# The recurrence of an RWKV-7 mixer in one Trainium2 kernel: factor matmuls laid on four quarters of the array, copies of T moved to ScalarE, factor steps two pairs ahead, the two directions interleaved phase by phase

## The reference

```python
def step(state, inp):
    r_t, w_t, k_t, v_t, kk_t, a_t = inp
    sk = jnp.einsum('bhij,bhj->bhi', state, kk_t)
    state = (state * w_t[:, :, None, :]
             - sk[..., :, None] * (kk_t * a_t)[:, :, None, :]
             + v_t[..., :, None] * k_t[:, :, None, :])
    y = jnp.einsum('bhij,bhj->bhi', state, r_t)
    return state, y
...
_, ys = lax.scan(step, s0, xs, reverse=reverse)
...
y = y + wkv7_scan(rh, hs(decay), kd, vh, kk, ah, reverse=(d == 1))
```

## Time and profile before

| | us |
|---|---|
| median of 3 runs (2830.68 to 2834.61) | 2833.74 |
| the profiled execution, its own time | 2847.62 |
| its span, first to last instruction | 2845.8 |
| mean granted TensorE clock, as a share of full | 0.963 |
| busy: TensorE / VectorE / ScalarE / POOL | 2624.5 / 1603.1 / 1137.7 / 917.4 |
| the recurrence, from its first transpose to its last step | 456 |

### The profile page before, as it was taken

One profiled execution on the slowest core, in us unless ns is written; L12 is line 12 of the kernel. 1 busy time (PEld: TensorE's weight loads), 2 busy tenths in 40 slices (PEclk: granted clock), 3 DMA queues, 4 the chain that ended last, 5 costly groups with the idle time before them and its releaser, 6 DMA issues. The chain is left out here.

```text
span 2845.8 us, 54939 instructions
## 1 busy us (share of the span) xinstructions
PE 2624.5 (92%) x23187; PEld 2156.2 (76%) x23187; DVE 1603.1 (56%) x2296; ACT 1137.7 (40%) x1802; POOL 917.4 (32%) x625
## 2 busy tenths in 40 slices
PE   5998999796999998979999999996897999999998
PEld 5776566576889988758888888885776888888887
DVE  7775522467565544666555565445655555556445
ACT  4211332553434332344444443554434444444434
POOL 1302122104112110225777770000412777773000
PEclk9999999898999998989999999998998999999999
DMA  6676433602211221322222227553122322225654
GB/s 232 229 270 214 168 133 155 205 18 80 76 47 48 82 80 32 126 72 76 89 75 81 89 90 276 171 169 109 53 90 73 89 89 74 82 89 216 190 182 144
DMA packets 295927, 346.48 MB, mean 122 GB/s; under 512 B 28383, under 2 KB 224212, under 8 KB 295684
## 3 DMA queue, kind: packets, MB, share of 16 engines
q1 hardware_dynamic: 286044, 336.64, 36.6%
q10 hardware_dynamic: 9640, 6.33, 0.7%
HBM read 271.58 MB, written 71.34 MB: 120 GB/s over the span
## 5 line engine op out<-in xcount | busy, mean ns | idle before, releaser
L2848 POOL TENSOR_TENSOR cg_u_lo<-cg_u_raw,cg_u_hi 128x512 fp32r<-128x512 f32 x210 | 314.9, 1507 | 147.2 <-ACT cg_u_hi L2734 147.2
L131 PE MATMUL cg_ps<-m_hi,cg_u_hi 128*128 128x512 f32 x844 | 331.1, 392 | 25.9 <-DVE cg_u_lo L2923 21.6
L133 PE MATMUL cg_ps<-m_hi,cg_u_lo 128*128 128x512 f32 x844 | 330.3, 391 | 0.0
L132 PE MATMUL cg_ps<-m_lo,cg_u_hi 128*128 128x512 f32 x808 | 315.8, 391 | 0.0
L2734 ACT ACTIVATE cg_u_hi<-cg_u_raw 128x512 fp32r<-128x512 f32 x216 | 132.1, 629 | 380.7 <-PE cg_ps L133 230.0
L131 PEld LDWEIGHTS cg_ps<-m_hi,cg_u_hi 128*128 128x128 f32 x844 | 159.8, 189 | 61.0 <-DVE cg_u_lo L2923 22.4
L131 PE MATMUL cg_ps<-over_y_tx,cg_u_hi 128*128 128x512 f32 x480 | 186.7, 389 | 0.0
L132 PE MATMUL cg_ps<-over_y_tx,cg_u_hi 128*128 128x512 f32 x480 | 186.7, 389 | 0.0
L133 PE MATMUL cg_ps<-over_y_tx,cg_u_lo 128*128 128x512 f32 x480 | 186.7, 389 | 0.0
L133 PEld LDWEIGHTS cg_ps<-m_hi,cg_u_lo 128*128 128x128 f32 x844 | 159.6, 189 | 33.5
L2900 DVE SCALAR_TENSOR_TENSOR cg_z<-cg_ps,top_conv_f,cg_z 128x1023 f32<-128x1023 f32 x88 | 112.9, 1283 | 115.3 <-ACT cg_z L2758 115.3
(11 more groups left out here) (475 smaller groups left out, 6515.2 us busy)
## 6 DMA issues: line engine op xcount, KB each, us to landing
cg_u_raw<-in_ffn_up SPq DMA_DIRECT2D x88, 512.0 KB, 5.1
cg_u_raw<-in_ffn_down SPq DMA_DIRECT2D x64, 512.0 KB, 5.0
qkv_mw<-in_ada_w SPq DMA_DIRECT2D x12, 2048.0 KB
over_f_d_raw<-in_ffn_down SPq DMA_DIRECT2D x48, 512.0 KB, 5.4
scr_act<-cg_z SPq DMA_DIRECT2D x44, 512.0 KB, 2.7
qkv_mw<-in_ada_w SPq DMA_DIRECT2D x8, 1024.0 KB, 11.3
next_w<-in_mix_in SPq DMA_DIRECT2D x16, 512.0 KB, 6.2
za_out<-in_ada_w SPq DMA_DIRECT2D x8, 1024.0 KB
```

The source lines that it names most:

```text
L131: nc.tensor.matmul(out, a_hi, b_hi, start=first, stop=False)
L132: nc.tensor.matmul(out, a_hi, b_lo, start=False, stop=False)
L133: return nc.tensor.matmul(out, a_lo, b_hi, start=False, stop=last)
L2848: G.tensor_tensor(u_lo[:, n % RING], source(g, i), u_hi[:, n % RING].bitcast(F32), ALU.subtract).then_inc(ulo_done, 1)
```

## The change

Every function gets a guard that makes it empty for a pair number outside 0 to 7 (left out below). The two heads of a tile get different homes: `home(c, u)` is `side(c)` for the units of head 0 and `other(c)` for those of head 1. X, values write to `home` from `side` or `other`; T and solve read at `home` and write to `side`; U reads and writes at `home`. PSUM is seen in units of 128 columns: X and T use `wide(g, 0)` (banks 0 and 1), U `wide(g, 1)` (banks 2 and 3), with head 0 in the first bank and head 1 in the second. Loops run over f, then hh, then c. Since U1 of head 1 is now needed at the other half, `lower` computes it once more there and VectorE copies it under a mask; `upper` is left with head 0. The alphas of head 1 lie in the other order, so VectorE makes them in two instructions.

```diff
+        pw = pb[:, :, :].rearrange("p k (f n) -> p (k f) n", n=P)
...
-        def alpha_of(g, m):
-            a = halves(st[m % 2][g][:, :, 0:P])
-            return a[:, :, ::-1, :] if g == 0 else a[:, :, :, ::-1]
+        def alpha_of(g, m, hh):
+            a = halves(st[m % 2][g][head(hh), :, 0:P])
+            a = a if g == 0 else a[:, :, :, ::-1]
+            return a[:, :, ::-1, :] if g == hh else a
+
+        def alpha_slot(c, hh):
+            return slice(((1 - c) ^ hh) * CH, (((1 - c) ^ hh) + 1) * CH)
+
+        def home(c, u):
+            return side(c) if u < KU else other(c)
+
+        def wide(g, r):
+            return pw[:, (2 * g + r) * UN:(2 * g + r + 1) * UN, :]
 
         def rho_of(g, m):
             a = st[m % 2][g][:, :, P:2 * P]
...
-        def narrow(g, k, b):
-            return bank(g, k)[:, 0:UN * HC].rearrange("p (u q b) -> p u q b", u=UN, b=b)
+        def narrow(g, r, b):
+            return wide(g, r)[:, :, 0:HC].rearrange("p u (q b) -> p u q b", b=b)
...
+            def load_lw(g, m):
+                if m < NPAIR:
                     sp.wait_ge(f_alpha[g], m)
+                    load(lw[g], lw_d[g][:, :, tokens_of(g, m)], rates_loaded[g])
+                    sp.wait_ge(f_nb[g], m)
+                    load(kk[g], kk_d[:, :, tokens_of(g, m)], f_loaded[g])
+
+            def load_aa(g, m):
+                if m < NPAIR:
                     sp.wait_ge(f_nbeta[g], m)
-                    sp.wait_ge(f_kd[g], m)
...
+            for m in range(-1, NPAIR):
+                if 0 <= m < NPAIR - 1:
+                    for g in range(2):
+                        if m:
+                            sp.wait_ge(rg_c[g], 2 * m)
+                        load_values(g, m + 1)
+                load_lw(0, m + 2)
+                load_aa(1, m + 2)
+                load_rx(1, m + 2)
+                load_lw(1, m + 2)
+                load_kx(1, m + 2)
+                load_aa(0, m + 2)
+                load_rx(0, m + 2)
+                load_kx(0, m + 2)
             for g in range(2):
                 for done in (f_alpha, f_nbeta, f_kappa, f_rho, f_ends):
                     sp.wait_ge(done[g], NPAIR)
...
                 for f in range(KU):
                     for c in range(2):
                         for hh in range(2):
                             nbeta = t[head(hh), f, 2 * P + CH + c * CH:2 * P + CH + (c + 1) * CH]
-                            ins = mm(bank(g, hh)[side(c), f * CH:(f + 1) * CH], t[head(hh), f, (1 - c) * CH:(2 - c) * CH], nbeta,
+                            ins = mm(bank(g, hh)[side(c), f * CH:(f + 1) * CH], t[head(hh), f, alpha_slot(c, hh)], nbeta,
                                      start=True, stop=True)
+                for f in range(KU):
+                    for c in range(2):
+                        nbeta = t[head(1), f, 2 * P + CH + c * CH:2 * P + CH + (c + 1) * CH]
+                        ins = mm(bank(g, 1)[other(c), (KU + f) * CH:(KU + f + 1) * CH], nbeta, t[head(1), f, alpha_slot(c, 1)],
+                                 start=True, stop=True)
                 ins.then_inc(l_done[g], 1)
 
...
                 pe.wait_ge(tok_c[g], 5 * m + 5)
-                for u in range(UN):
-                    hh, f = divmod(u, KU)
-                    for c in range(2):
-                        ins = mm(bank(g, 2)[side(c), u * CH:(u + 1) * CH], xn[g][other(c), hh, 2 * f + c, 0:CH], wv[g][other(c), c, u, :],
-                                 start=True, stop=True)
+                for f in range(KU):
+                    for hh in range(2):
+                        u = hh * KU + f
+                        for c in range(2):
+                            ins = mm(bank(g, 2 + hh)[home(c, u), f * CH:(f + 1) * CH], xn[g][other(c), hh, 2 * f + c, 0:CH],
+                                     wv[g][other(c), c, u, :], start=True, stop=True)
                 ins.then_inc(mv_done[g], 1)
 
...
-                for u in range(UN):
-                    hh, f = divmod(u, KU)
-                    for c in range(2):
-                        out = bank(g, 3)[side(c), u * HC:(u + 1) * HC].rearrange("p (q b) -> p q b", b=b)
-                        ins = mm(out, xn[g][side(c), hh, 2 * f + c, 0:CH], cols1(src[side(c), u, :], b, 0), start=True, stop=True)
+                for f in range(KU):
+                    for hh in range(2):
+                        u = hh * KU + f
+                        for c in range(2):
+                            out = wide(g, 0)[home(c, u), u, 0:HC].rearrange("p (q b) -> p q b", b=b)
+                            ins = mm(out, xn[g][side(c), hh, 2 * f + c, 0:CH], cols1(src[side(c), u, :], b, 0), start=True, stop=True)
                 ins.then_inc(x_done[g], 1)
 
-            def level_tu(g, m, i):
...
+                for f in range(KU):
+                    for hh in range(2):
+                        u = hh * KU + f
                         for c in range(2):
                             if i == 0:
-                                out, x = bank(g, 0)[side(c), u * CH:(u + 1) * CH], XL[i][g][side(c), u, :]
+                                out, x = wide(g, 0)[side(c), u, 0:CH], XL[i][g][home(c, u), u, :]
                             else:
-                                out = bank(g, 0)[side(c), u * HC:(u + 1) * HC].rearrange("p (q b) -> p q b", b=b)
-                                x = cols1(XL[i][g][side(c), u, :], b, 0)
-                            ins = mm(out, old[side(c), u, :], x, start=True, stop=True)
-                    ins.then_inc(t_done[g], 1)
+                                out = wide(g, 0)[side(c), u, 0:HC].rearrange("p (q b) -> p q b", b=b)
+                                x = cols1(XL[i][g][home(c, u), u, :], b, 0)
+                            ins = mm(out, old[home(c, u), u, :], x, start=True, stop=True)
...
+                            out, y = wide(g, 1)[home(c, u), u, 0:CH], old[home(c, u), u, :]
                         else:
-                            out = bank(g, 1)[side(c), u * HC:(u + 1) * HC].rearrange("p (q b) -> p q b", b=b)
-                            y = cols1(old[side(c), u, :], b, 1)
-                        ins = mm(out, XL[i][g][side(c), u, :], y, start=True, stop=True)
+                            out = wide(g, 1)[home(c, u), u, 0:HC].rearrange("p (q b) -> p q b", b=b)
+                            y = cols1(old[home(c, u), u, :], b, 1)
+                        ins = mm(out, XL[i][g][home(c, u), u, :], y, start=True, stop=True)
                 ins.then_inc(u_done[g], 1)
 
...
-                for u in range(UN):
-                    hh, f = divmod(u, KU)
-                    for c in range(2):
-                        ins = mm(bank(g, 2 + hh)[side(c), f * P:(f + 1) * P], U[g][side(c), u, :], rz[g][side(c), u, :],
-                                 start=True, stop=True)
+                for f in range(KU):
+                    for hh in range(2):
+                        u = hh * KU + f
+                        for c in range(2):
+                            ins = mm(bank(g, 2 + hh)[side(c), f * P:(f + 1) * P], U[g][home(c, u), u, :], rz[g][home(c, u), u, :],
+                                     start=True, stop=True)
                 ins.then_inc(z_done[g], 1)
 
...
```

T and U become phases of their own, `step` is cut in `step_open` (what doesn't depend on the state) and `step_close`, `turn` and `scores` in two parts each; `level_t` of VectorE is dropped and ScalarE has it. TensorE's order:

```diff
-            for m in range(NPAIR):
-                for phase in (turn, scores, lower, values):
-                    for g in range(2):
-                        phase(g, m)
-                for i in range(NL):
-                    for g in range(2):
-                        level_x(g, m, i)
-                    for g in range(2):
-                        level_tu(g, m, i)
-                for phase in (solve, carry):
-                    for g in range(2):
-                        phase(g, m)
-                for c in range(2):
-                    for g in range(2):
-                        step(g, m, c)
+            for m in range(NPAIR + 1):
+                turn(0, m, 0)
+                turn(1, m, 0)
+                turn(0, m, 1)
+                step_close(1, m - 1, 1)
+                scores(0, m, 0)
+                scores(0, m, 1)
+                turn(1, m, 1)
+                scores(1, m, 0)
+                lower(0, m)
+                scores(1, m, 1)
+                values(0, m)
+                level_x(0, m, 0)
+                lower(1, m)
+                level_t(0, m, 0)
+                level_u(0, m, 0)
+                level_x(0, m, 1)
+                values(1, m)
+                level_x(1, m, 0)
+                level_t(0, m, 1)
+                level_u(0, m, 1)
+                level_t(1, m, 0)
+                level_u(1, m, 0)
+                level_x(1, m, 1)
+                level_x(0, m, 2)
+                level_t(1, m, 1)
+                level_t(0, m, 2)
+                level_u(1, m, 1)
+                level_x(1, m, 2)
+                level_u(0, m, 2)
+                level_t(1, m, 2)
+                level_x(0, m, 3)
+                level_u(1, m, 2)
+                level_t(0, m, 3)
+                level_x(1, m, 3)
```

(115 more changed lines are left out.)

317 lines of the change are left out of this document (202 added, 115 removed).

## The result

The changed kernel takes 2870.2 us (median of 4 runs, 2863.0 to 2879.7), the kernel before, run beside it, 2834.2; the ratio is 1.012 [1.010, 1.015]. The forecast was 2753.

A forecast was written before the change was run, and what follows sets the result against it. TensorE's issue was taken as the bound: 22 us later start, 1.5 cold start, 1.1 last close and eight pairs of 43.9 make 375.8 for 456.0, 80 less; with the median's offset 2753, range 2725 to 2795.

The forecast's parts named there:

- PE's rate: TensorE issue: each quarter takes an instruction each 55 to 60 ns; four quarters give 14 ns where two give 29.
- term of -10.0 us a pair: PE issue per pair: values 0.9, X 4.7, T 3.8, solve 1.5 less, `lower` 0.9 more.
- the prediction's pair: One pair of the recurrence: best 54.4 less 10.0, less 1.5, plus 1.0 is 43.9 us, bounds 41 and 48.
- three signs of being wrong: X or T groups staying at 1.03 us, a pair over 48 us, or a start costing under 10 us.
- The floor as a rival: Issue floor between 14 and 29 ns in the four-quarter phases: 4.8 us a pair, 38 in all, 2791; chance 0.04.
- rule of the Trainium skill: TensorE start-to-start never below about 25 ns; values, X and T stay 11 ns above `lower`'s rate, result 2809.
- rule on weight loads: Loads overlap only when row group differs; T and solve keep their rate: 42 us, 2795; chance 0.06.
- Clock: Mean pair's excess over the best, 2.6 us, goes without the hole ahead of T; otherwise up to 2 us a pair.
- Idle time and the order: Waits in a pair: other direction's phases cover copies, so idle falls from 3.5 to 2.0 us, 1.5 less.
- Latency as a rival: PE waits at ScalarE's or VectorE's copies, half a us at ten level phases: +5 a pair, 2793; chance 0.14.
- Factor steps and T copies: ScalarE 25.6, VectorE about 29 us a pair, free beside PE; lost cover costs 0.5 us on each engine.
- The start: Iteration -1 precedes pair 0's first copies: first masked scores at 692, start 22 us later, bounds 14 and 28.

The follow-up runs named there:

- e1: TensorE streams alone, two or four quarters, 32 to 128 columns; with 64 columns on four, 128 loads each 3.45 us, 27 ns a load.
- e9: TensorE streams alone on four quarters, with no-operations or 24 transfers of 512 KB beside; 128 loads each 6.2 us beside transfers, 3.45 without.
- e6_places4: e5_places with the factors on four quarters and the added instructions of `lower`; 2842.4 us, 1.001 of the kernel before.
- e5_places: Changed kernel with factors on two quarters, alphas in old order, factor steps one pair ahead at earlier, reordered places; 2824.5 us, 0.995 of the kernel before.
- e4_quarters: Kernel before with the factors on four quarters and what `lower` needs; order, T copies and factor steps as before; 2846.4 us, 1.003.
- e8_t_act: Kernel before with the T copies moved from VectorE to ScalarE, nothing else; 2838.2 us, 1.001.
- e10_t_dve: e5_places with the T copies back on VectorE, nothing else; 2857.5 us, 1.007 of the kernel before.
- e2_two: Changed kernel with factors back on two quarters, without the added `lower` work; order, T copies, two pairs' notice stay; 2844.9 us, 1.002 of the kernel before.
- e7_order: e2_two with the alphas of the second head in their old order; 2847.1 us, 1.004 of the kernel before.

## Why the prediction was wrong

**PE's rate.** This is the step that failed: "So a quarter takes an instruction each 55 to 60 ns ... and the number of quarters in use sets the rate." The 14 ns was read from `lower`, a group of 32 loads, and was true for groups (0.56 us for 32 X loads after). It was then used for a stretch: values, five levels of X and U and four of T are 64 x 15 = 960 loads a pair, seven and a half blocks. A rate that outruns the supply holds for what is in stock, some 180 to 310 loads behind a slow stretch or an idle one (e1, e9), and behind that only the supply counts: 27 ns a load at best (3.45 us for 128), 29 to 32 in e6_places4. The term of -10.0 us a pair was worth about nothing: 15.7 against 16.2 us in the stretch at a clock of 1.00, and 51.8 against 52.1 for the best pairs of e6_places4 and e5_places. With -0.5 in its place the prediction's pair comes to 53.4 us and not 43.9. (By its own count X is 4.8 us and not 4.7, a slip that changes nothing.) Of its three signs of being wrong only the pair of over 48 us came: X and T did run at 0.56 us for 32, in short groups.

**The floor as a rival** came nearest, and was refused with "`lower` itself speaks against it", a burst against a floor. The rule of the Trainium skill (TensorE: Matmul & The Clock Gate, section "Wait — 56ns, not 53.3ns?") that start-to-start never drops below about 25 ns doesn't agree with the single start, 14 ns here before and after. It is close to the mean behind the stock, 27 ns in e1_micro's section with 64 columns. The estimate by it, 2809, would still have been 61 us short. Its rule on weight loads (the same page, packing small matmuls), that they overlap only when the row group differs, would keep T and solve at their old rate. The trace doesn't agree: 29 loads of T, with rows in the order 1,0,0,1, took 0.55 us, 15 ns each, and 41 of solve 1.31 us (1066.94 on), 29 ns each where 53 were needed before.

**Clock.** "Without the hole I let it go", with "up to 2 us a pair" as its price. The new stops are holes too, and a fall in the late levels lasted until `solve`: 20 us of the pair at 853.7 lie at 1.2 GHz, where the pairs before have 0 to 7. I put the 18 us by which e6_places4 lies above e5_places down to this and to the instructions added to `lower`; no run parts the two.

**Idle time and the order.** Right in kind. T's wait for the masked copy fell as forecast (13.6 to 0.7 us, and idle ahead of T is 3.3 in e5_places), the pairs on two quarters take 52.1 to 53.6 us in e5_places with the clock at 1.00, where the best one before took 54.4. Latency as a rival is what e4_quarters shows in the old order: a faster engine waits longer for the same copies.

**Factor steps and T copies.** ScalarE's 25.6 us a pair and VectorE's 29 are as worked out (25.7 and 28.9). The T copies by themselves are worth nothing in the old order, as said (e8_t_act). In the new one it is worth 33 us to have them off VectorE (e10_t_dve); "their work costs nothing while it is beside PE" was too easy there.

**The start.** Right in kind and nearly in size: 22 us forecast. The first scores wait for ScalarE's `tokens`, and these for iteration -1:

```profile
664.40 4.24 PE L1550 MATMUL rw_pb<-top_ident,rw_st 128*128 128x128 f32 x20 [28.55 <-DVE rw_st L2128]
...
671.94 1.65 ACT L1856 ACTIVATE rw_kd<-att_aa,rw_rest_ka,top_vec 128x128 f32<-128x128 f32 x4 [19.05 <-DMA att_kx<-scr_z]
...
683.82 3.79 PE L1568 MATMUL rw_pb<-rw_st 64*128 64x128 f32 x32 [14.74 <-ACT rw_xn L1787]
...
689.36 1.28 DVE L2005 TENSOR_TENSOR rw_xn<-rw_pb,rw_causal 128x512 f32<-128x512 f32 x2
```

The masked scores begin at 689.4 (forecast 692; 672.5 before), and the first pair exceeds a mean one by 22.3 us (78.6 less 56.3). Part of that is the clock, 0.69 in this pair, so the agreement is in part luck; e2_two has 20 us at 0.87 and e7_order 27 at 0.78. Without iteration -1 it exceeds it by 4 (e5_places, 56.9, and 52.8 for the mean of the next five). This is where the gain of the order went in the changed kernel: e7_order has it and gives it back at the start.

**The sum, mended,** by the medians: the late start and the new order, with the T copies on ScalarE, +7 and +9 us (e2_two and e7_order against the kernel before), in which some 22 us of start stand against 2.3 to 3 us for each of seven pairs (53.5 for 55.8 in e8_t_act, and for 56.5 in the trace before); four quarters, with what `lower` needs for them and what the clock does, +25 to +29 (the changed kernel against e2_two). Together +32 to +38, measured +36.

## What to carry to other kernels

A rate read from a short group is a burst; ahead of using it for a stretch, count the instructions of the stretch and set them against what the instruction queue has shown it can bring (here 128 load and matmul pairs each 3.45 us, each 6.2 beside full DMA queues). Idle time in the middle of a phase with "issue" behind it, each 128 loads, is how such a limit looks. Where the clock falls, look 1 to 2 us ahead of the fall for the wait, and at the engine that was late for it. Where work is already at 29 ns, the way to less time is fewer instructions, or their order, not more of the array; and a step that is moved a pair ahead is also moved ahead of everything at the start, so move it within the pair first.

## What the runs showed of the hardware that was not expected

- Instructions of TensorE come in blocks of 16,384 bytes over one DMA queue; a block lasts 128 load and matmul pairs, takes 1.0 to 1.2 us on the queue and came no sooner than each 3.4 us where the stock was used up (3.4 to 4.0 in the changed kernel, 3.45 to 4.0 in e1_micro, 6.2 with 397 GB/s beside it in e9_micro2).
- TensorE stayed at 1.2 GHz through 39 us of gapless work with 32 columns on two quarters; it was back at 2.4 GHz after 5.3 us with 64 columns on two, and after 3.6 us with 32 columns on four (e1_micro).
- On four quarters with 64x64 tiles a load and its matmul start each 14 to 15 ns with 32 and with 64 columns alike, until the stock is used (e1_micro: 182 loads in 2.79 us, 272 in 4.06).
- A scan of VectorE's and a product of POOL's that begin within 0.2 us of each other don't both keep their time: the one that began second took 1 us longer, 2.17 to 2.25 us for 1.22 (scan) and 2.20 to 2.27 for 1.26 (product), in all seven cases of e10_t_dve.
